# A two-block transformer program: routing intermediates out of PSUM, the mask matmuls of the mLSTM regrouped, and two output projections swapped

## The reference

```
s = einsum('thcd,hcnd->thcn', q, sub_keys)
s1, i1 = top_k(s[:, :, 0], 16);  s2, i2 = top_k(s[:, :, 1], 16)
cand_s = s1[..., :, None] + s2[..., None, :]          # 16 x 16 sums
top_s, top_pos = top_k(cand_s, 16)                    # and the expert indices behind them
gates = softmax(top_s)
out = sum over k of gates * gelu(u[expert] . x) * v[expert]
```

```
y_ret = (silu(rg) * rms(retention)) @ w_ret_out
y_na = neighbourhood_attention @ w_na_out
merged = sigmoid(g_ret) * y_ret + sigmoid(g_na) * y_na
return merged @ w_out
```

## Time and profile before

| | before |
|---|---|
| median of 3 runs | 2755.65 us (2755.16 to 2756.26) |
| profiled execution | 2755.65 us |
| its span, first to last instruction | 2753.1 us |
| mean granted TensorE clock | 0.986 of full speed |
| PE busy | 2661.9 us (97%) |
| PEld busy | 2357.5 us (86%) |
| DVE busy | 1595.2 us (58%) |
| ACT busy | 1397.4 us (51%) |
| POOL busy | 559.8 us (20%), nearly all while `u` tiles stream |
| DMA | 447.58 MB, 163 GB/s mean |

### The profile page before, as it was taken

The page is one execution under the profiler, slowest core; times in us unless marked ns, Lnnn a source line. Parts: engine busy times, 40 slices in busy tenths (PEclk is TensorE's granted clock), DMA queues, the critical chain, the costliest instruction groups (busy, mean ns, idle before and its releaser), DMA issues.

```text
span 2753.1 us, 46306 instructions
## 1 busy us (share of the span) xinstructions
PE 2661.9 (97%) x16714; PEld 2357.5 (86%) x16714; DVE 1595.2 (58%) x2858; ACT 1397.4 (51%) x2310; POOL 559.8 (20%) x325
## 2 busy tenths in 40 slices
PE   8999999999999998999999999999989999988998
PEld 7789999998888875789999998888869978766996
DVE  3558746675555553449556765555555646535664
ACT  4434567664544544344577654544545445443543
POOL 0006876640000000008866630000000000000000
PEclk9999999999999999999999999999999999999999
DMA  6245544446566553245544446555546555434454
GB/s 212 77 147 175 183 156 144 140 145 202 192 192 195 191 169 100 85 145 184 183 147 142 142 153 203 192 195 192 191 141 204 183 160 184 130 94 144 155 182 151
DMA packets 124034, 447.58 MB, mean 163 GB/s; under 512 B 14280, under 2 KB 14920, under 8 KB 123648
## 3 DMA queue, kind: packets, MB, share of 16 engines
q1 hardware_dynamic: 119808, 434.16, 48.6%
q0 software_dynamic: 2608, 9.08, 1.1%
q10 hardware_dynamic: 1488, 2.59, 0.3%
HBM read 444.74 MB, written 1.05 MB: 162 GB/s over the span
## 4 chain that ended last, share of the span: by engine, by line
PE 92%; DVE 5%; ACT 2%; issue 1%; DMA 1%; ACTq 0%; DVEq 0%
PE ps L710 40%; PE ps L682 14%; PE ps L688 14%; PE ps L685 14%; PE ps L862 4%; PE ps L660 1%; DVE X L1544 1%; PE ps L918 1%; PE ps L833 1%; DVE big L1544 1%; PE ps L742 1%; DVE x_lo L1591 0%; DVE stats L1624 0%; PE ps L748 0%; DVE X L1620 0%
## 5 line engine op out<-in xcount | busy, mean ns | idle before, releaser
L388 ACT CAST w_hi<-ring 128x1024 fp32r<-128x1024 f32 (+1 forms) x808 | 846.0, 1047 | 1016.6 <-PE ps L710 559.4
L400 DVE TENSOR_TENSOR w_lo<-ring,w_hi 128x1024 fp32r<-128x1024 f32 (+1 forms) x640 | 782.5, 1223 | 844.4 <-ACT w_hi L388 834.5
L682 PE MATMUL ps<-x_hi,w_hi 128*128 128x256 f32 x3136 | 781.0, 287 | 3.1 <-DVE x_lo L1596 2.7
L685 PE MATMUL ps<-x_lo,w_hi 128*128 128x256 f32 x3136 | 768.4, 283 | 0.0
L682 PEld LDWEIGHTS ps<-x_hi,w_hi 128*128 128x128 f32 x3136 | 600.2, 191 | 6.5 <-issue 4.9
L685 PEld LDWEIGHTS ps<-x_lo,w_hi 128*128 128x128 f32 x3136 | 601.0, 192 | 0.1
L400 POOL TENSOR_TENSOR w_lo<-ring,w_hi 128x1024 fp32r<-128x1024 f32 x168 | 403.8, 2404 | 580.8 <-ACT w_hi L388 580.8
L688 PE MATMUL ps<-x_hi,w_lo 128*128 128x256 f32 x3136 | 440.2, 283 | 0.0
L710 PE MATMUL ps<-w_hi,x_hi 128*128 128x512 f32 x1488 | 410.3, 394 | 16.4 <-DVE x_lo L1591 12.7
L710 PE MATMUL ps<-w_hi,x_lo 128*128 128x512 f32 x1488 | 404.8, 391 | 0.0
L688 PEld LDWEIGHTS ps<-x_hi,w_lo 128*128 128x128 f32 x3136 | 404.5, 192 | 0.0
(11 more groups left out here) (235 smaller groups left out, 1992.4 us busy)
## 6 DMA issues: line engine op xcount, KB each, us to landing
ring<-in_u SPq DMA_DIRECT2D x256, 512.0 KB, 3.4
ring<-in_v SPq DMA_DIRECT2D x256, 512.0 KB, 3.6
ring<-in_ffn_in SPq DMA_DIRECT2D x88, 512.0 KB, 3.5
ring<-in_ffn_out SPq DMA_DIRECT2D x44, 512.0 KB, 3.4
ring<-in_wq SPq DMA_DIRECT2D x32, 512.0 KB, 3.5
ring<-in_ple_gate SPq DMA_DIRECT2D x16, 512.0 KB, 3.6
SC<-in_rows POOLq DMA_DIRECT2D x11, 512.0 KB, 4.9
ring<-in_a_qk SPq DMA_DIRECT2D x8, 512.0 KB, 4.5
```

Of the source, the lines that this page charges most:

```text
L388: nc.scalar.copy(part(w_hi, i)[:, used(name)], tile(i)[:, used(name)]).then_inc(tiles_hi, 1)
L400: eng.tensor_tensor(part(w_lo, i)[:, at], tile(i)[:, at], part(w_hi, i)[:, at], ALU.subtract).then_inc(tiles_low[LOW[n][0]], 1)
L682: mm = nc.tensor.matmul(bank(s)[:, 0:T], hi[:, k, :], x_hi[:, k, :], start=(k == 0), stop=False)
L685: nc.tensor.matmul(bank(s)[:, 0:T], hi[:, k, :], x_lo[:, k, :], start=False, stop=False)
```

## The change

It has three independent parts. First, `TIf`, `firsts` and `HL` leave PSUM: `TIf` becomes an in-place conversion of `TI` in SBUF, `HL` goes to a free stretch of `SC`, and `firsts` is dropped (the sums read `TV` twice). Second, `ml_first` adds the mask to each of the two decay products right behind it and computes the scores last. Third, in the mixing `ret_out` comes before `na_out`, in the stream, in `acc` and in all engines' lists; the square root comes before `g_na`'s sigmoid, its table is loaded before the last two casts of the last head, `ret_out`'s first tile is split early, and the merged turn's fillers wait for `na_out`.

```diff
-           ... "merged": (8, "ret_out"), "rms3": (40, "mix_out")}
+           ... "merged": (8, "na_out"), "rms3": (40, "mix_out")}
-    + [("na_out", 4), ("ret_out", 8), ("mix_out", 8)]
+    + [("ret_out", 8), ("na_out", 4), ("mix_out", 8)]
...
-        TIf = shaped(ps[:, 1, :], TB, 2 * H8, TOPK)
-        firsts = shaped(ps[:, 2, :], TB, 2 * H8, TOPK)
+        TIf = shaped(tops[:, 512:1024], TB, 2 * H8, TOPK)
-        HL = shaped(ps[:, 0, :], 2, TB, H8, TOPK)
+        HL = shaped(SC[:, 2816:3328], 2, TB, H8, TOPK)
...
 def ml_first(h):          # TensorE
-    decay[0:T]     = ml_sel x ml_rows          (8 rows)
-    decay[T:T+P]   = ml_sel x ml_rows          (8 rows)
-    scores[0:T]    = k x q                     (64 rows)
-    scores[T:T+P]  = k x q                     (64 rows)   -> scores full
-    decay[0:P]    += ident x ml_mask           (128 rows)
-    decay[T:T+P]  += ident x ml_mask           (128 rows)  -> decay full
+    decay[0:T]     = ml_sel x ml_rows          (8 rows)
+    decay[0:P]    += ident x ml_mask           (128 rows)
+    decay[T:T+P]   = ml_sel x ml_rows          (8 rows)
+    decay[T:T+P]  += ident x ml_mask           (128 rows)  -> decay full
+    scores[0:T]    = k x q                     (64 rows)
+    scores[T:T+P]  = k x q                     (64 rows)   -> scores full
...
 # TensorE, end of the mixing
-            moved(pe, SLOT[("na", "out", H8 - 1)])
-            to_acc("na_out", tokens(na_oT), 4)
             turn_over("ret", ret_y.rearrange("p t h n -> p t (h n)"))
             moved(pe, SLOT["turn_ret"], 4)
             split_to_acc("ret_out")
+            moved(pe, SLOT[("na", "out", H8 - 1)])
+            to_acc("na_out", tokens(na_oT), 4)
             turn_over("merged", merged)
 # ScalarE
-                    take_high(act, "g_na", 2 * h + 1)
+                    sqrt_table()
+                    highs("g_na", 2 * h + 1, 2 * h + 2, following="ret_out")
...
             act.sem_inc(sums_ready, 1)
+            square_roots(8)
             from_acc("g_na", lambda tb: sig_na[:, tb, :], ACT.Sigmoid)
-            square_roots(8)
-            take_high(act, "ret_out", 0)
             turned_parts("ret")
             highs("ret_out", 1, 8)
+            acc_here(act, "na_out")
             take_high(act, "mix_out", 0)
 # VectorE, routing
-                step(V.tensor_copy(firsts, TV))
-                    tt(c, v(firsts, tb)[:, :, 0, :, None]..., v(TV, tb)[:, :, 1, None, :]..., ALU.add)
+                    tt(c, v(tb)[:, :, 0, :, None]..., v(tb)[:, :, 1, None, :]..., ALU.add)
 # VectorE, end of the mixing
             by_halves(gated_retention)
-            acc_moved_up_to("g_na", TB - 1)
-            gated_from("na_out", merged, sig_na)
-            take_low(dve, "ret_out", 0)
             turned_parts("ret")
             lows("ret_out", 1, 8)
-            gated_from("ret_out", merged_tmp, sig_ret)
-            acc_moved_up_to("ret_out", TB - 1)
+            for name, dst, gate in (("ret_out", merged_tmp, sig_ret), ("na_out", merged, sig_na)):
+                (gate both halves of the tokens out of acc)
+            acc_moved_up_to("na_out", TB - 1)
             by_halves(lambda tb, at: tt(merged[:, tb, at], merged[:, tb, at], merged_tmp[:, tb, at], ALU.add))
```

More of the change, by code:

```diff
@@ L74 @@
 FILLERS = {"ml_out": (24, "a_og"), "ln0_0": (28, "a_out"), "x1": (12, "ple_gate0"), "ln1_0": (28, "b_out"),
-           "rms1": (40, "ple_gate1"), "rms2": (40, "ffn1_out"), "merged": (8, "ret_out"), "rms3": (40, "mix_out")}
+           "rms1": (40, "ple_gate1"), "rms2": (40, "ffn1_out"), "merged": (8, "na_out"), "rms3": (40, "mix_out")}
 FILLERS_AFTER = 8
@@ L96 @@
              "v1", "ple_proj1", "ple_gate1", "ffn1_out", "rqk", "rv", "rg", "nv", "g_ret", "g_na",
-             "na_out", "ret_out", "mix_out", "ffn2_out"]
+             "ret_out", "na_out", "mix_out", "ffn2_out"]
 TURN_ORDER = ["ml_out", "ln0_0", "ln0_1", "x1", "ln1_0", "ln1_1", "x2", "rms1", "rms2", "rqk", "ret", "merged", "rms3"]
@@ L780, in ml_first @@
             def ml_first(h):
[L782 to L787, removed]
-                r, q, k = head_rows(h), h // 2, 4 + h // 2
[L789 to L793, removed]
+                s = SLOT[("ml", "decay", h)]
+                slot_free(pe, s)
+                nc.tensor.matmul(bank(s)[:, 0:T], ml_sel[0:H8, h, :], ml_rows[0:H8, 7, :], start=True, stop=False)
+                nc.tensor.matmul(bank(s)[:, 0:P], ident[:], ml_mask[:], start=False, stop=True)
+                nc.tensor.matmul(bank(s)[:, T:T + P], ml_sel[0:H8, h, :], ml_rows[0:H8, 7, P:T],
+                                 start=True, stop=False)
+                full(nc.tensor.matmul(bank(s)[:, T:T + P], ident[:], ml_mask[:], start=False, stop=True), s)
+                s = SLOT[("ml", "scores", h)]
+                slot_free(pe, s)
+                r, q, k = head_rows(h), h // 2, 4 + h // 2
+                nc.tensor.matmul(bank(s)[:, 0:T], ml_qk[r, k, 0:P], ml_qk[r, q, :], start=True, stop=True)
+                full(nc.tensor.matmul(bank(s)[:, T:T + P], ml_qk[r, k, P:T], ml_qk[r, q, P:T],
+                                      start=True, stop=True), s)
             moved(pe, SLOT["a_qk"], 8)
@@ L1789, in routing @@
                 step(V.tensor_copy(TIf, TI))
-                step(V.tensor_copy(firsts, TV))
                 wait()
-                v = lambda t, tb: t[:, tb].rearrange("p (h c) k -> p h c k", c=2)
+                v = lambda tb: TV[:, tb].rearrange("p (h c) k -> p h c k", c=2)
                 c = shaped(SC[:, 0:2048], H8, TOPK, TOPK)
                 for tb in range(TB):
-                    tt(c, v(firsts, tb)[:, :, 0, :, None].to_broadcast([P, H8, TOPK, TOPK]),
-                       v(TV, tb)[:, :, 1, None, :].to_broadcast([P, H8, TOPK, TOPK]), ALU.add)
+                    tt(c, v(tb)[:, :, 0, :, None].to_broadcast([P, H8, TOPK, TOPK]),
+                       v(tb)[:, :, 1, None, :].to_broadcast([P, H8, TOPK, TOPK]), ALU.add)
                     wait()
@@ L2149, in _ @@
                 else:
-                    lows("g_na", 2 * h + 1, 2 * h + 2)
+                    lows("g_na", 2 * h + 1, 2 * h + 2, following="ret_out")
             mean_square_roots(2 * RET_H, T, RMS_EPS, src=3)
@@ L2161, in _ @@
             by_halves(gated_retention)
-            def gated_from(name, dst, gate):
+            turned_parts("ret")
+            lows("ret_out", 1, 8)
+            for name, dst, gate in (("ret_out", merged_tmp, sig_ret), ("na_out", merged, sig_na)):
                 for tb in range(TB):
@@ L2167, in gated_from @@
                     V.tensor_tensor(dst[:, tb, :], gate[:, tb, :], acc_rows(tb), ALU.mult).then_inc(acc_moved, 1)
-            acc_moved_up_to("g_na", TB - 1)
-            gated_from("na_out", merged, sig_na)
-            take_low(dve, "ret_out", 0)
-            turned_parts("ret")
-            lows("ret_out", 1, 8)
-            gated_from("ret_out", merged_tmp, sig_ret)
-            acc_moved_up_to("ret_out", TB - 1)
+            acc_moved_up_to("na_out", TB - 1)
             by_halves(lambda tb, at: tt(merged[:, tb, at], merged[:, tb, at], merged_tmp[:, tb, at], ALU.add))
```

## The result

| | before | after |
|---|---|---|
| median of the comparison | 2755.40 us (4 runs) | 2785.66 us (4 runs, 2785.09 to 2786.64) |
| ratio, 95% interval | | 1.0113 [1.0096, 1.0131] |
| profiled execution | 2755.65 us | 2789.65 us |
| its span | 2753.1 us | 2786.9 us |
| mean granted clock | 0.986 | 0.984 |

The change makes the kernel 30.3 us slower (interval 26.5 to 36.1), where 29.7 was forecast. The profiled execution of the changed kernel is 4 us above its median; its mean granted clock is 0.984, where the other four runs have 0.986.

What follows compares the result with a forecast made beforehand. TensorE, 92% of the chain, was taken to bound the kernel. 24.0 + 4.8 + 0.9 = 29.7 on 2755.65 gave 2785 us; forecast 2778 to 2794 (chance 0.70), range 2765 to 2797.

Steps and rivals of the forecast that it cites:

- Edit 1: Routing intermediates in SBUF: VectorE and GpSimd exclude each other at the shared port, TensorE waits; 12.0 a layer, +24.0 us.
- Edit 2: mLSTM heads: three more changes of row number per head at 0.20 us, eight heads, +4.8 us; bounds 1.6 and 6.
- Edit 3: Tail with ret_out first: table load +1.4, mix_out nearer -1.7, table load behind mix_out +1.2; sum +0.9, from -3 to +5.
- the 10.1 case: Routing's four groups of compare, product, reduction: GpSimd gets a second w_lo beside the reduction, TensorE 10.1 us late per layer.
- The sums: Routing's two lone sums of TV per layer: each makes TensorE wait 0.6 us, 1.2 a layer.
- The groups: Routing's four groups of compare, product, reduction: engines alternate, 10.8 us a layer, taken between 10.1 and 11.5.
- the rival of growing stalls: TensorE's waits between u tiles let the clock fall, or VectorE keeps the port for two; 2800 us, chance 0.09.
- the first rival: The port costs nothing because GpSimd's delay stays inside 0.95 us of slack; +5.7, 2761 us, chance 0.13.
- Cover: After routing, VectorE's 30.77 us of idle time hides its own lengthening of some 24 us.
- the lower bound of 1.6: mLSTM heads: if the unseen change from 8 to 128 rows were free, 8 x 0.20 = 1.6 us is left.
- The weight load by row groups: mLSTM heads: weights load beside a running matmul only when row groups differ; +0.8 instead of +4.8, 2781 us, chance 0.04.
- The rearranged tail wins: Tail: both idle stretches and both low starts go, 13.5 at most, -10.9 with the costs; 2749.6 us, chance 0.04.

Runs made afterwards that it cites:

- In halves: Edit 1 alone, with each candidate sum, compare and product of 2048 elements issued as two of 1024; 1.0061, +16.8 us against the kernel before.
- Edit 2 alone: Only the new order of the decay, mask and score matmuls in ml_first, on the kernel before; 1.0032, +8.8 us.
- eight rows: Edit 2 alone, but the mask matmuls read only 8 rows of the identity and of the mask; 0.9996, -1.1 us against the kernel before.

## Why the prediction came out

The forecast of 2785 against 2785.66 is nearer than its terms were. That the main term came right is its mechanism; that the sum came within 1 us is luck. Edit 1 was put 1.3 too high by the marks (2.8 by the timing alone), Edit 2 3 to 4 too low, Edit 3 1 to 2 too low. The parts measured one by one sum to 33.0, not 30.3; the difference lies inside their intervals.

- **Edit 1, +24.0: shown, 22.7 in the two traces' marks, +21.2 timed alone.** The mechanism is as put: both engines exclude each other for a whole instruction and take turns. It follows the number of SBUF pairs (10, 6 and 2 operations: 22.8, 11.2, 2.5 us in B and C together) and goes with the length of a turn. The Trainium skill has the exclusion for a whole instruction, in SBUF — State Buffer, "Who interferes with whom", and all these traces agree. That the turns alternate, and what a turn costs TensorE, is read from the rows of this case: VectorE's operations read 4.3 to 4.4, `w_lo` 10.94 for three; the 10.1 case (GpSimd gets a second `w_lo` beside the reduction) is the one that came. Inside the term two errors nearly cancel. The sums were put at 1.2 a layer and cost 1.9: one falls 0.93 late, and the gap around each wait was not counted. The groups were put at 10.8, between the two cases, and cost 9.5 to 9.8.
- **The bounds**: TensorE's clock stayed at 1.00 through all the waits of up to 1.25 us, so the rival of growing stalls falls. The port's price is not 0, so the first rival falls too.
- **Cover**: VectorE's idle time behind routing went from 30.77 only to 28.11 us, since TensorE came later as well. VectorE was put some 24 us longer; in layer 0 it finished 14.1 us later, counted from the fillers ahead of `ln0_0`. A wait of 4.73 us for ScalarE that it had behind the last reduction (ahead of L1831) was gone, and the two sums took 2.29 and 2.60 where up to 4.6 was put. In halves the cover ran out.
- **Edit 2, +4.8: the mechanism shown, the term mis-sized.** The gaps cost 0.59 a head, 4.7 in eight, to the 0.60 forecast. The change from 8 to 128 rows, the one not seen before, costs what the others do, so the lower bound of 1.6 was not needed. What the term left out is the clock: the timed cost of 8.8 (5.5 to 12.1) has its middle above the upper bound of 6 and holds it at its edge. Both traces with six changes show low stretches in the heads behind the first, two with Edit 2 alone and three in the changed kernel, at 1.6 to 1.8 us each. I had put the clock beside the port's waits, where it did nothing, and not here, where TensorE never shows an idle time.
- **The weight load by row groups** falls: every warm head, even or odd, lost 0.59 with Edit 2, and none with eight rows, though the masks' rows 0 to 7 overlap the decay's in both. The Trainium skill, TensorE: Matmul & The Clock Gate, "The mechanism", hides a weight load only where row groups differ; here it is a change of the number of rows that costs, overlapping or not, and equal, overlapping rows run 0.22 apart.
- **Edit 3, +0.9: timed +3.0 (0.6 to 5.2), its middle inside the bounds of -3 to +5; by the marks (G and D) +1.8 alone and +2.2 in the changed kernel.** The wait at tile 7 came as put (1.49 against 0.18, +1.3). `mix_out` comes 0.9 to 1.3 nearer instead of 1.7: `ret_out` starts 11.87 behind the last retention product where 11.3 was put, and it and `na_out` took 0.3 longer each. The norm behind `mix_out` lost the 1.2 that was put, and 0.6 more to the clock. The low start of `ret_out` stayed, as the sum had it.
- **The rearranged tail wins**: not as changed. Once the table loads and the low starts are taken out it does, by 6.6 timed and 5.7 in D. Fillers in the old order bring 4.4 timed (1.9 to 7.2) and 2.5 in D. So the traces leave some 3 us for the new order with its loads and its first `mix_out` tile placed anew, and the timings alone, whose intervals overlap, don't show it.

## What to carry to other kernels

Two buffers in SBUF under one VectorE `tensor_tensor` were not free here while GpSimd worked on SBUF: each such operation of 2048 elements held GpSimd off for some 2 us, its whole length, and one PSUM operand avoided it; what it costs is the hold less what the waiting engine idles anyway, counted per turn. On TensorE, order matmuls of few and of many rows so that the number of rows changes seldom, 0.20 us a change here, and remember that small gaps that never show as idle may cost the clock too. When a piece of work is moved ahead of a table load or a wait, price its other half: here the order itself was worth little, and where the loads and fillers stood was worth more.

## What the runs showed of the hardware that I had not expected

- TensorE at the low clock, 1.2 GHz, while it is 100% busy by the profile: 0.57 of full speed from 88 to 92 us with Edit 2 alone, behind matmuls that start 0.1 to 0.2 us further apart at each change of rows; with equal rows 1.00 in the same heads. The waits of 1.25 us in the `u` tiles did not do this (42.30 of 50 us busy from 308 to 358, clock 1.00).
- A wait on TensorE costs more than its length: 0.16 to 0.25 us in the tile that waits, 0.10 in the next (1.50 late for a wait of 1.25, 0.90 for 0.74, and 0.10 behind each).
- The clock scatters where nothing was changed: between the fillers of `x1` and those of `ln1_0` the kernels took from 125.9 to 131.3 us for the same work, which is as much as most terms here.
